# A streaming encoder layer with product-key experts: eight ScalarE scalings of one-hot rows become one GpSimd multiply, placed among the gathers

## What is computed

```
q = (xb @ w_q)                                  # 8 heads, two halves of a key each
v1, i1 = top_k(s1, 16); v2, i2 = top_k(s2, 16)  # 128 sub-keys each
top_s, sel = top_k(v1 + v2, 16)                 # of 256 pairs; expert number = i1 * 128 + i2
g = softmax(top_s)
act = gelu(einsum("thkd,td->thk", u_tab[eidx], xb))
out = einsum("thk,thkd->td", g * act, v_tab[eidx])   # 8 * 16 = 128 experts for each token
```

## Time and profile before

| | before |
|---|---|
| median of 3 runs | 1904.15 us (1901.82 to 1912.47) |
| profiled execution, its own time | 1894.53 us |
| its span in the profile | 1892.3 us |
| TensorE busy | 1461.6 us (77%) |
| VectorE busy | 1440.3 us (76%) |
| ScalarE busy | 647.2 us (34%) |
| GpSimd busy | 798.9 us (42%) |
| mean DMA rate | 357 GB/s |

### The profile page before, as it was taken

One profiled execution on the slowest core, in us unless ns is written; L12 is line 12 of the kernel. 1 busy time (PEld: TensorE's weight loads), 2 busy tenths in 40 slices (PEclk: granted clock), 3 DMA queues, 4 the chain that ended last, 5 costly groups with the idle time before them and its releaser, 6 DMA issues.

```text
span 1892.3 us, 17663 instructions
## 1 busy us (share of the span) xinstructions
PE 1461.6 (77%) x4810; PEld 798.8 (42%) x4810; DVE 1440.3 (76%) x2954; ACT 647.2 (34%) x1962; POOL 798.9 (42%) x667
## 2 busy tenths in 40 slices
PE   6779978878850662429328899999997999999997
PEld 5555533444430531217215555433334555433332
DVE  1376587699999789887989999997666667566666
ACT  4314553333331131000017777212114667411112
POOL 2022333433356888888863434332222344322220
PEclk9889989998975876669669999999998899999999
DMA  9489899998898999999988899999997899999997
GB/s 358 149 319 370 338 391 394 384 384 323 353 343 288 365 404 383 347 355 356 333 332 310 329 338 336 410 416 417 416 417 279 317 352 347 372 417 416 417 417 292
DMA packets 146483, 675.80 MB, mean 357 GB/s; under 512 B 15216, under 2 KB 15472, under 8 KB 97232
## 3 DMA queue, kind: packets, MB, share of 16 engines
q0 software_dynamic: 92832, 538.39, 73.4%
q1 hardware_dynamic: 50496, 132.68, 18.4%
q10 hardware_dynamic: 3056, 3.61, 0.5%
HBM read 671.61 MB, written 3.01 MB: 357 GB/s over the span
## 4 chain that ended last, share of the span: by engine, by line
DMA 31%; DVE 25%; PE 24%; issue 13%; ACT 4%; POOL 3%; ACTq 0%; DVEq 0%; POOLq 0%; SPq 0%
DMA ring<-experts,idc 21%; DMA arena<-experts 9%; PE accY L1452 9%; DVE ring L880 8%; PE pb L1437 4%; PE pb L1426 3%; DVE ring L872 3%; POOL ring L596 3%; PE pb L1257 2%; DVE xt L889 2%; ACT arena L1183 1%; PE pq L1383 1%; PE pb L1275 1%; DVE idx L800 1%; DVE arena L931 1%
## 5 line engine op out<-in xcount | busy, mean ns | idle before, releaser
L594 POOL DMA_INDIRECT ring<-experts,idc x384 | 444.6, 1158 | 966.8 <-PE accY L1452 457.3
L872 DVE CUSTOM_DVE_ANT_0 ring<-ring,h 128x1024 f32<-128x1024 f32 x384 | 466.7, 1222 | 287.2 <-DMA ring<-experts,idc 286.3
L1452 PE MATMUL accY<-ring,diag 128*128 128x512 f32 x896 | 453.0, 647 | 91.5 <-ACT diag L1169 81.3
L1437 PE MATMUL pb<-arena 128*128 128x512 f32 x1024 | 470.8, 605 | 14.9 <-DMA arena<-experts 8.2
L596 POOL DMA_INDIRECT ring<-experts,idc x256 | 344.2, 1344 | 86.4 <-issue 76.5
L880 DVE CUSTOM_DVE_ANT_0 ring<-ring,h 128x1024 f32<-128x1024 f32 x256 | 304.9, 1224 | 58.8 <-DMA ring<-experts,idc 57.3
L1437 PEld LDWEIGHTS pb<-arena 128*128 128x128 f32 x1024 | 185.8, 190 | 298.2 <-issue 193.7
L1158 ACT ACTIVATE ge<-zt 128x1 f32<-128x1 f32 x384 | 76.6, 200 | 673.7 <-DVE zt L872 673.1
L1452 PEld LDWEIGHTS accY<-ring,diag 128*128 128x128 f32 x896 | 172.9, 204 | 290.6 <-issue 165.8
L889 DVE SCALAR_TENSOR_TENSOR xt<-ring,coef,xt 128x1024 f32<-128x1024 f32 x160 | 204.9, 1281 | 3.1 <-ACT coef L1162 3.0
L1383 PE MATMUL pq<-arena 128*128 128x256 f32 (+1 forms) x768 | 152.3, 357 | 46.8 <-ACT arena L1153 36.5
(11 more groups left out here) (173 smaller groups left out, 1105.5 us busy)
## 6 DMA issues: line engine op xcount, KB each, us to landing
arena<-experts SPq DMA_DIRECT2D x128, 512.0 KB, 15.1
arena<-w_q SPq DMA_DIRECT2D x12, 2048.0 KB, 19.4
arena<-w_in SPq DMA_DIRECT2D x11, 2048.0 KB, 18.8
ring<-experts,idc POOLq DMA_INDIRECT x640, 8.7
arena<-w_out SPq DMA_DIRECT2D x4, 2048.0 KB, 18.7
ring<-w_out SPq DMA_DIRECT2D x2, 2048.0 KB, 20.0
xt<-x_all SPq DMA_DIRECT2D x5, 512.0 KB, 13.5
y_all<-xt ACTq DMA_DIRECT2D x5, 512.0 KB, 3.0
```

The costliest lines, as they stand in the source:

```text
L594: nc.gpsimd.indirect_dma_start(ring[:, at // 2], None, experts, index).then_inc(gat[at], 16)
L872: V.tensor_tensor_reduce(out=half(g), in0=half(g), in1=h2[:], scale=1.0, scalar=0.0, op0=ALU.mult, op1=ALU.add, accum_out=zt[:, s % 8:s % ...
L1437: ins = T.matmul(pb[:, 2 * j + k], cm[:, i, j * P:(j + 1) * P], vring[:, n % VRING, k * 512:(k + 1) * 512], start=i == 0, stop=i == BLOCKS ...
L1452: ins = T.matmul(accY[:, j], diag[:, (n - 1) % DIAGS], ring[:, place, D + j * 512:D + (j + 1) * 512], start=first, stop=final)
```

## The change

The eight ScalarE scalings of a fill are replaced by one GpSimd `tensor_tensor` multiply over the same 128 x 512 elements, in place, with the coefficient broadcast over 64 elements. GpSimd now walks through a list of its own, `POOL_ORDER`. It holds the gathers in their old order and each multiply behind the gathers of three more `dot` items than `ORDER` has in front of that fill. VectorE's and TensorE's programs do not change.

```diff
+def pool_order():
+
+    made, held = [], []
+    for item in ORDER:
+        if item[0] in ("dot", "udot"):
+            made.append(("whole" if item[0] == "dot" else "u", item[1]))
+            held = [(left - 1, fill) for left, fill in held]
+            while held and held[0][0] <= 0:
+                made.append(held.pop(0)[1])
+        if item[0] == "fill":
+            held.append((3, item))
+    assert [g for g in made if g[0] != "fill"] == GATHERS
+    return made + [fill for _, fill in held]
...
-            for g in GATHERS:
+            def gather(g):
...
+            def scale_hot(h, n):
+
+                k = BATCHES * h + n
+                pool.wait_ge(hot_done, k + 1)
+                pool.sem_inc(pool_held, 1)
+                c = idT[:, 2, n * BATCH:(n + 1) * BATCH].unsqueeze(2).to_broadcast([P, BATCH, BLOCKS])
+                nc.gpsimd.tensor_tensor(hot1[:, k % 2], hot1[:, k % 2], c, ALU.mult).then_inc(hot_scaled, 1)
+
+            for item in POOL_ORDER:
+                if item[0] == "fill":
+                    scale_hot(item[1], item[2])
+                else:
+                    gather(item)
...
-            def scale_hot(h, n):
-                k = BATCHES * h + n
-                a.wait_ge(hot_done, k + 1)
-                for i in range(BATCH):
-                    ins = A.activation(hot1[:, k % 2, i], hot1[:, k % 2, i], ACT.Copy,
-                                       scale=idT[:, 2, n * BATCH + i:n * BATCH + i + 1])
-                ins.then_inc(hot_scaled, 1)
-
...
                 elif item[0] == "fill":
-                    scale_hot(item[1], item[2])
                     if item[2]:
                         keep(item[1], item[2] - 1)
```

More of the change, by code:

```diff
@@ L168 @@
            + [("whole", s) for s in range(SLOTS, WHOLE)])
+def pool_order():
[10 more added lines that the diff above has]
+    return made + [fill for _, fill in held]
+POOL_ORDER = pool_order()
 def ring_places():
```

## The result

The changed kernel takes 1920.24 us (median of 16 runs, 1908.62 to 1928.53), the kernel before 1906.13 us in its 16 runs (1892.79 to 1914.18). The ratio is 1.0073, 95% interval 1.0049 to 1.0097: 14 us slower, clear of no change by the interval and, at 0.73%, just over the 0.5% that the prediction named as the bound. The profiled executions took 1912.48 us and 1894.53 us. The one of before was 11.6 us under its median, the one of after 7.8 us under its own, so a difference between the two traces overstates the change by some 4 us.

A forecast was written before the change was run, and what follows sets the result against it. In the fill stages no engine alone was full; gathers, VectorE and TensorE's waits set the round. Terms of +2, +12 and +9 us on 1894.5 gave 1917.5, plus 9.6 to the median: 1927 us, range 1898 to 1957.

The forecast's parts named there:

- ScalarE's relief: Fill stages: taking the scalings from ScalarE gives nothing; at most 17 us if other work did not cover it.
- the hold: Fill stages: the multiply blocks VectorE's two-input instructions, 1.10 us in 14 fills of stage 1; 9 us there, 2 in stage 2.
- The one-sided-port rival: Fill stages: the multiply waits for VectorE but never holds it; +5 us, 1909 us, chance 0.20.
- The quick multiply: Fill stages: the multiply finds its gap and TensorE's waits shrink; 1892 us, faster, chance 0.15.
- The dear multiply: Fill stages: the multiply takes 2.0 us or loses the port to several instructions; +50 us, 1954 us, chance 0.13.
- The late gathers: Fill stages: gathers issued later because they stand behind the multiply; 3 us in stage 1, 7 us in stage 2.
- the loop: Fill stages: dot d, one-hots, multiply, gather d+4, landing, dot d+4; 2.96 + multiply + 0.3 + 5.6 to 8.0 us for four slots.
- 2 + 12 + 9 = 23 us: Whole kernel: +2 us for the two starts, +12 for fill stage 1, +9 for fill stage 2.
- the starts: Beginning of both fill stages: an early gather now goes behind the multiply; nearly hidden, 1 us each, +2 us.
- The two numbers of stage length: Sign of being right: fill stages of about 209 and 206 us, block stages as before.
- a changed granted clock: Sign of being wrong: fill stages' granted clock moves from 0.97 and 0.92.

The follow-up runs named there:

- wait and multiply: Kernel before, ScalarE still scaling; GpSimd waits for the one-hot rows, then makes a same-size multiply between unused weight tiles: 1912.92 us, ratio 1.0067.
- Multiply without wait: Kernel before, ScalarE still scaling; GpSimd makes a same-size multiply between unused weight tiles, without waiting for VectorE: 1917.76 us, ratio 1.0087.
- memsets without reads: Kernel before, ScalarE still scaling; two GpSimd memsets of 512 elements at each place, no wait for VectorE: 1897.73 us, ratio 0.9993.
- The copy without wait: Kernel before, ScalarE still scaling; one GpSimd copy of 512 elements at each place, no wait for VectorE: 1910.07 us, ratio 1.0046.
- The wait alone: Kernel before, ScalarE still scaling; GpSimd only waits for the one-hot rows at the change's places and multiplies nothing: 1895.52 us, ratio 0.9984.

## Why the prediction was right, and where it was not

**Place and direction: right.** The time is lost in the fill stages, the block stages neither lose nor win it back, and nothing that shows comes back from ScalarE's relief. The last is shown by the run with wait and multiply beside ScalarE's scalings: the same time as the changed kernel.

**Cause: right in the main.** The two engines hold each other up, in both directions. Multiply without wait: +0.87%. Same time in memsets without reads: nothing. In that pair no gather stands behind a wait for the one-hots, so the hold costs time by itself. The one-sided-port rival falls by the 24 stretched instructions (its 1909 us is not far from the time measured). The quick multiply falls: TensorE's waits did not shrink, and 10 of the 64 multiplies end within 1.3 us of the one-hots, where I had 19. The dear multiply falls too; 1.04 us undisturbed against my 1.10.

**The hold: nearly exact.** I had 14 instructions held for 1.10 us in stage 1; there are 15, held 0.74 us on the mean, since most multiplies had first waited for a dot and had 0.97 us to go when the next instruction began. For stage 2 I had 2 us, against 6.8 us of held time. Together that is 17.4 us forecast and 17.8 found, with the two stages off in opposite ways. In the sum the holds stood for 11 us (9 + 2). The copy without wait, with as much held time (19.5 us) and no gather late, costs 9 us (4 to 14 by its interval).

**The late gathers: priced at 10 us, and not settled.** I counted a fifth and six tenths of them, 3 + 7 us of the 23. The wait alone costs nothing (-0.35% to +0.03%). Adding the wait to the multiply did not make it dearer (0.67% after 0.87%), but it also took held time away (18.3 us after 43.4), so this does not price them. The trace of the changed kernel shows the loop at work:

```profile
1513.39 3.65 PE L1475 MATMUL accY<-ring,diag 128*128 128x512 f32 x8
...
1516.41 1.90 POOL L622 TENSOR_TENSOR arena<-arena,qT 128x512 f32<-128x512 f32 x1 [2.53 <-DVE arena L965]
...
1518.47 0.98 POOL L612 DMA_INDIRECT ring<-experts,idc  x1 [0.15 <-issue]
...
1526.29 1.23 DVE L904 CUSTOM_DVE_ANT_0 ring<-ring,h 128x1024 f32<-128x1024 f32 x1 [2.56 <-DMA ring<-experts,idc]
```

The addition that frees the place is the first half of the first row, over at about 1515.3. The gather goes 3.1 us later, behind the multiply, and VectorE then stands 2.56 us waiting for it. VectorE so waits for a gather that the multiply had made late in 23 of 62 fills (7 in stage 1, 16 in stage 2; with the wait alone in 11). The waits, each counted at most as long as the gather was late, sum to 32 us (10 us with the wait alone). That is no sum of losses: the wait-only run lost nothing by its 10 us, and VectorE's idle time in the two stages went from 69.1 only to 73.9 us, less than with the memsets (78.9; table below). How much of it is a loss, no run here shows. A gather held for wait and multiply without any read, for example by wait and memsets, was not tried. What the copy leaves over, 14 less 9, is 5 us, and the intervals are as wide as that.

**Where the 14 us lie.** From the start of the first to that of the last `hot1` one-hot of each fill stage, VectorE does the same instructions in every one of these runs. Stage length is its busy time and its idle time (us, single profiled executions):

| | stage 1: length = busy + idle | stage 2: length = busy + idle |
|---|---|---|
| before | 184.0 = 172.4 + 11.6 | 184.9 = 127.4 + 57.5 |
| memsets | 191.6 = 173.1 + 18.5 | 187.7 = 127.3 + 60.4 |
| copy, no wait | 194.1 = 182.6 + 11.5 | 191.6 = 137.5 + 54.1 |
| multiply, no wait | 204.6 = 191.4 + 13.2 | 195.5 = 150.8 + 44.7 |
| wait and multiply | 201.2 = 184.8 + 16.4 | 190.7 = 135.4 + 55.3 |
| changed kernel | 202.0 = 185.8 + 16.2 | 191.7 = 134.1 + 57.7 |

Against the memsets, which cost nothing, the changed kernel is 10.4 and 4.0 us longer, about the 14 us measured, and VectorE is busy 12.7 and 6.8 us longer. (The profiled execution of the memsets lies 1.5 us above its median, that of the changed kernel 7.8 us under its own.) The multiply without wait shows why a held microsecond has no fixed price. In stage 1, where VectorE has little idle time, 18.3 us more of busy time cost 13.0. In stage 2, where it stands waiting for landings for 60 us, 23.5 us cost 7.8, and the rest went into those waits.

**The sum.** 2 + 12 + 9 = 23 us against 14 measured. The holds stood in it for 11 us, which the runs bear out (9 by the copy, 14 if nothing else cost). So the excess lies in the starts and the late gathers, 2 + 10 us, for which 5 us at most is left by the middle values. The mis-sized term is the late gathers. The two numbers of stage length that I gave as a sign, 209 and 206 us, came out as 209 and 207, and that is luck, since the profiled execution of before had a short stage 1.

**Open.** Stage 1 grew by 18 us from first to last one-hot and stage 2 by 7, with 11.1 and 6.8 us held. The harmless runs (wait alone, memsets) both show 191.6 us for stage 1 where before shows 184.0, so part of the 18 is a quick stretch of one execution of before; how much is left open. I had named a changed granted clock as a sign of being wrong. It did change in stage 1, 0.91 after 0.97, but the harmless runs show 0.93 there at no cost, and in stage 2 it went the other way (0.94 after 0.92) while the time was lost there too. That stage 1 grew in VectorE's busy time speaks against the clock as the cause of the rest, but no run separates it.

## What to carry to other kernels

An idle engine is no free engine. Ask whether an instruction reads while another engine reads two inputs: here a multiply of 1.04 us on GpSimd waited for VectorE's two-input instructions and then held them, mostly for 0.83 us, while memsets of the same length cost nothing. What held time costs depends on the slack of the engine that is held. Before moving work to shorten a wait, look whether its latency can be put beside other work where it is; swapping two VectorE instructions gave 0.64%, with every engine's work unchanged. And a place in an in-order queue is a dependency in both directions: one gather later made the kernel 5.4% slower than before and one earlier 3.8%, where the place chosen made it 0.7%.

## What the runs showed of the hardware that I had not expected

- The hold on VectorE ends just ahead of the end of the GpSimd instruction. In all 24 stretched instructions of the changed kernel, and in all 273 of the six other runs with a multiply on GpSimd and a hold, the VectorE instruction takes its undisturbed time counted from 0.13 or 0.14 us ahead of the multiply's end. So a multiply that had to wait for a dot, and has 0.97 us to go, holds the next instruction for 0.83 us; a copy, 0.61 us long undisturbed, mostly holds it for 0.40 us, and a memset of 512 (0.54 us) not at all. The longer holds, 1.55 us in the changed kernel and several at 1.23 us beside the multiply without wait, fit this too: there the record of the VectorE instruction begins ahead of the multiply's. Why VectorE is the one that waits in those cases I did not find out, and seven of the copy's 51 do not fit.
- Eight one-input VectorE instructions of 64 elements with two scalars for each partition took 1.87 us busy (0.30 us each by the records, which overlap), almost three times the one broadcast instruction over the same 512 elements (0.68 us).
